# Moving seven of eight expert routings of each token tile one gather phase later

## The reference, cut to what matters

```
scores = q . sub_keys            # per token, 8 heads, two halves of 128 keys
top_s, top_i = top_k(scores, 16) # per half
cand = top_s[0] + top_s[1]       # 16 x 16 candidates
best_s, best_j = top_k(cand, 16) # 16 experts of a head
experts = i1 * 128 + i2 ; gates = softmax(best_s)
act = gelu(h . u_tab[experts])   # 128 experts of a token
x += sum_k gates * act * v_tab[experts]
```

## Time and profile before

| | us |
|---|---|
| median of 3 runs | 1702.29 (1701.94 to 1702.77) |
| span of the profiled execution | 1697.8 |
| its own time | not given apart from the span; the median lies 4.5 above the span |
| PE busy | 1314.6 (77%) |
| DVE busy | 1285.1 (76%) |
| POOL busy | 685.6 (40%) |
| ACT busy | 319.0 (19%) |
| DMA moved | 623.23 MB, mean 367 GB/s |

### The profile page before, as it was taken

The page is one execution under the profiler, slowest core; times in us unless marked ns, Lnnn a source line. Parts: engine busy times, 40 slices in busy tenths (PEclk is TensorE's granted clock), DMA queues, the critical chain, the costliest instruction groups (busy, mean ns, idle before and its releaser), DMA issues.

```text
span 1697.8 us, 15521 instructions
## 1 busy us (share of the span) xinstructions
PE 1314.6 (77%) x4636; PEld 737.9 (43%) x4636; DVE 1285.1 (76%) x3347; ACT 319.0 (19%) x932; POOL 685.6 (40%) x791
## 2 busy tenths in 40 slices
PE   7884875877686787877878778879878778787777
PEld 6663442443354344544355434545345433333332
DVE  3835999966599987878589987978679985555555
ACT  2221111122211121212121121123121111111111
POOL 6002233586285343534332243435432334445542
PEclk9897897988798888989988989889979988999989
DMA  9007998969998899999999989999999989999997
GB/s 390 9 28 291 388 367 311 397 251 384 413 383 313 313 420 420 419 420 420 420 380 420 387 330 420 420 420 415 420 389 420 369 309 421 420 420 421 420 421 309
DMA packets 86053, 623.23 MB, mean 367 GB/s; under 512 B 9808, under 2 KB 9808, under 8 KB 10960
## 3 DMA queue, kind: packets, MB, share of 16 engines
q0 software_dynamic: 73728, 536.90, 77.8%
q1 hardware_dynamic: 12240, 85.33, 12.3%
HBM read 621.15 MB, written 1.05 MB: 366 GB/s over the span
## 4 chain that ended last, share of the span: by engine, by line
DVE 42%; DMA 23%; PE 20%; issue 4%; POOL 3%; ACT 1%; DVEq 0%; POOLq 0%; ACTq 0%
DMA slot<-experts,idx 23%; DVE slot L1041 15%; PE acc L1350 12%; DVE work L760 6%; PE PX L1293 2%; DVE work L973 2%; POOL slot L458 2%; DVE ge L760 2%; DVE xs L1061 2%; PE PB L1168 1%; DVE ex L1013 1%; PE PB L1320 1%; DVE work L848 1%; DVE ti L981 1%; DVE ti L979 1%
## 5 line engine op out<-in xcount | busy, mean ns | idle before, releaser
L1350 PE MATMUL acc<-slot,diag 128*128 128x512 f32 x1780 | 874.8, 647 | 227.6 <-ACT diag L734 227.5
L458 POOL DMA_INDIRECT slot<-experts,idx x512 | 587.9, 1148 | 970.2 <-PE acc L1350 806.2
L1041 DVE CUSTOM_DVE_ANT_0 slot<-slot,h 128x1024 f32<-128x1024 f32 x512 | 611.2, 1226 | 238.7 <-DMA slot<-experts,idx 236.9
L1350 PEld LDWEIGHTS acc<-slot,diag 128*128 128x128 f32 x1780 | 359.7, 208 | 692.8 <-issue 421.6
L734 ACT ACTIVATE diag<-cst,ge 128x128 f32<-128x128 f32 x445 | 144.1, 391 | 269.6 <-DVE ge L1056 269.6
L1320 PE MATMUL PB<-hT,ring 128*128 128x128 f32 x1024 | 126.7, 285 | 5.6 <-ACT hT L698 4.1
L1320 PEld LDWEIGHTS PB<-hT,ring 128*128 128x128 f32 x1024 | 123.3, 201 | 7.6 <-ACT hT L698 5.5
L725 ACT ACTIVATE ge<-ge 128x4 f32<-128x4 f32 x129 | 26.5, 205 | 482.9 <-DVE ge L760 481.1
L1061 DVE SCALAR_TENSOR_TENSOR xs<-slot,ge,xs 128x1024 f32<-128x1024 f32 x67 | 86.3, 1288 | 2.4
L1168 PE MATMUL PB<-ring,hT 128*128 128x256 f32 x192 | 49.8, 418 | 16.9 <-DVE work L760 16.9
L1293 PE MATMUL PX<-ring,work 128*128 128x512 f32 x96 | 47.6, 642 | 15.0 <-DVE work L950 15.0
(11 more groups left out here) (231 smaller groups left out, 1197.3 us busy)
## 6 DMA issues: line engine op xcount, KB each, us to landing
ring<-weights SPq DMA_DIRECT2D x32, 1152.0 KB, 9.8
ring<-weights SPq DMA_DIRECT2D x28, 1024.0 KB, 9.2
slot<-weights SPq DMA_DIRECT2D x12, 1024.0 KB, 21.5
slot<-experts,idx POOLq DMA_INDIRECT x512, 14.9
sml<-small SPq DMA_DIRECT2D x2, 1160.0 KB, 9.2
xs<-x SPq DMA_DIRECT2D x2, 512.0 KB, 7.9
out<-xs SPq DMA_DIRECT2D x4, 256.0 KB, 5.2
tabp<-tabs SPq DMA_DIRECT2D x2, 268.0 KB, 7.9
```

Of the source, the lines that this page charges most:

```text
L458: pool.indirect_dma_start(out=slot[:, E % SLOTS, :], out_offset=None, in_=experts, in_offset=bass.IndirectOffsetOnAxis(ap=idx[:, n % 2, e: ...
L1041: ins = dve.tensor_tensor_reduce(u, u, h2[:, n % 2, :], 1.0, 0.0, ALU.mult, ALU.add, d[:, i:i + 1])
L1350: ins = pe.matmul(acc[:, half, :], diag[:, d % DIAGS, :], slot[:, E % SLOTS, D + half * 512:D + half * 512 + 512], start=(E % PICKS == 0), ...
```

## The change

`MIX1` ends with `route0`. The routings 1 to 7 of step n are placed at the beginning of phase n, ahead of the mixing of step n+1. For step 1 they carry `tab4` to `tab7` and `bT` with them (`ROUTES1`), so these run in phase 1. In phases 0 to 2 all rows are now placed within the first LEAD = 27 quads and the last five quads have none. In phase 3 the seven routings stand in quads 0, 2, 5, 8, 11, 14 and 17 (`ROUTE_AT`).

```diff
-        ("out0",), ("out1",), ("out2",), ("out3", "x1"), ("h2T", "rp"), ("route0",), ("route1",),
-        ("route2", "tab4"), ("route3", "tab5"), ("route4", "tab6"), ("route5", "tab7"), ("route6", "bT"),
-        ("route7",))
+        ("out0",), ("out1",), ("out2",), ("out3", "x1"), ("h2T", "rp"), ("route0",))
 ROUTES = tuple((f"route{h}",) for h in range(1, PH))
+
+ROUTES1 = (("route1",), ("route2", "tab4"), ("route3", "tab5"), ("route4", "tab6"), ("route5", "tab7"),
+           ("route6", "bT"), ("route7",))
+ROUTE_AT = (0, 2, 5, 8, 11, 14, 17)
+LEAD = QUADS - 5
...
-        if n == 0:
-
-            rows = [(0, r) for r in ROUTES] + [(1, r) for r in MIX1]
-        else:
-            rows = [(n + 1, r) for r in MIX + ROUTES] if n + 1 < STEPS else []
+
+        rows = [(n, r) for r in (ROUTES1 if n == 1 else ROUTES)]
+        if n + 1 < STEPS:
+            rows += [(n + 1, r) for r in (MIX if n else MIX1)]
...
-            while at < len(rows) * (quad + 1) // QUADS:
+            due = min(len(rows), len(rows) * (quad + 1) // LEAD) if n + 1 < STEPS else sum(q <= quad for q in ROUTE_AT)
+            while at < due:
```

## The result

The changed kernel takes **1717.72 us** (median of four runs, 1711.07 to 1722.77), the kernel before 1702.12 in the same session (1699.90 to 1702.77). The ratio is 1.0093, 95% interval 1.0068 to 1.0119: slower by 15.6 us, where 14 us less were forecast. Every run after is above every run before. The profiled execution is the run of 1722.77, with a span of 1721.0 us, 23.2 above the span before; that run is the slowest of the four, so the medians say 15.6 and the two traces 23.

A forecast was written before the change was run, and what follows sets the result against it. No engine passes 77%, so DMA time lost below 420 GB/s decides: 88.9 us instead of 103.6, 14.7 less, span 1683.1 from 1697.8, plus 4.5 for the median: 1687.6, said as 1688 us; own range 1679 to 1696, overall 1668 to 1702.

The forecast's parts named there:

- The removed run of phase 0: End of phase 0: one routing, then five bare quads keep DMA full, so the loss of 23.8 us goes to 0.
- The start of phase 0, and tab0 to tab3: New bare quads 0 and 13 cut the start's loss from 21.7 to 17.3 us; the tab0 to tab3 stretch keeps 20.7.
- The runs at the start of phases 1 and 2: Routings at each phase's start leave DMA idle: 18 us in phase 1 with tab4 to tab7, 11 in phase 2.
- The tighter mixing: Phases 1 and 2: 24 rows in 21 quads, so three quads hold two rows, delaying PE's additions; 6.5 us per phase.
- quad 26: h2T, rp0, then the scores and next rp in one quad: addition starts 5 us later; 3 us more per phase.
- quad 13: PE's y waits for the same quad's back rotation, with qkv3 behind it; 3 us per phase, ends 0 and 6.
- quad 20: Turn of heads 6 and 7 waits for DVE, with two quads, 20 us, in flight; 0.5 us per phase.
- Phase 3: Seven routings two or three quads apart stay DMA-paced: loss 0, old 16.6 us goes; five more chunks lengthen it 14 us.
- rival C: The gain is spent in phase 3: each routing there idles DMA 2 us, 14 come back, 1702 us; chance 0.08.
- B: Six quads with two rows in phases 1 and 2 idle DMA 7 us each: 1717; turning at 4.6; chance 0.10.
- All three conditions: Phase 3 windows below 410 GB/s; a POOL gather waiting much over 20 us at quad 13, 20 or 26; phase 1 dip over 24.
- A: Quads with two rows cost nothing and the POOL pieces hide: losses fall to 69 us, time 1668; chance 0.22.

The follow-up runs named there:

- single rows: The change, with phases 1 and 2 laid out one row a quad from quad 7 on (route7 and normA still share quad 6): 1688.51 us, ratio 0.9923.
- the first experiment: Against the kernel before, only step 3's seven routings moved into phase 3; phase 2 has mixing alone, one row a quad: 1689.85 us, ratio 0.9931.

## Why the prediction was wrong

**The removed run of phase 0: right.** 23.8 to 0 was forecast; the window 500 to 565 has 420 GB/s, and the end of the phase, 545, came at 545.62.

**The start of phase 0, and tab0 to tab3: nearly right.** 17.3 and 20.7 were forecast; 351 GB/s over 120 us are 19.7, and 21.3. The phase lost 44.4 where 40.4 was forecast; the 4 us did not show in its end.

**The runs at the start of phases 1 and 2: place right, size too small.** 18 and 11 were forecast, 25.5 and 15.4 measured. Quad 0 took 23.8 us from weights to weights at phase 1 and 23.3 at phase 2, where 19.9 was worked out, though its drain waits no more, as forecast; those 3.4 us are most of the 4.4 that the plain run lost beyond the 11. They lie in the dots: the last of the four ends 12.1 us after the weights at phase 2 and 11.8 at phase 1, where 8.9 was taken, with 5.8 and 4.7 us of waiting for landings between them. Why the gathers land that late there stays open. And such a run is moved by the change, not taken away: the three of before lost 23.8, 11.9 and 16.6, together 52.3; those of after, with all that phase 3 loses, 25.5, 15.4 and 9.8, together 50.7. The timeline of DVE in the kernel after, at the drain and at the CAST beside the coefficient pieces, and that of POOL beside the CAST:

```profile
558.10 1.41 DVE L764 TENSOR_TENSOR xs<-xs,acc 128x512 f32<-128x512 f32 x2
...
598.66 6.27 DVE L1007 CAST tif<-ti 128x32 f32<-128x32 uint32 x1
```

```profile
598.40 2.05 POOL L435 TENSOR_TENSOR work<-rot 128x512 f32<-128x512 f32 x2
...
602.43 2.47 POOL L435 TENSOR_TENSOR rot<-rot,work 128x512 f32<-128x512 f32 x2
```

The CAST of the earlier trace rows is there again with 6.27 us. The Trainium skill ("SBUF — State Buffer", section "SBUF: two separate sides") says that whichever of the two starts first gets the shared port pair for its whole instruction and the other fully blocks; the pair of 2.35 us beside two dots agrees. The CAST agrees in kind, but it did not take its turn behind one instruction: it ends only with the last of six GpSimd operations in a row, 598.40 to 604.90. The prediction's "in turn" is not what this row shows. The sum by that rule to the letter was 10 us above mine for the pieces. The run came out 7.5 above, but plain runs were 4.3 above as well, and taking the pieces out of the run gave 12.0 where I had taken 10, so the surplus that is theirs is nearer 2 than 10.

**The tighter mixing: here the prediction failed.** The step that failed is the price of "PE must finish both before it adds the last quad's experts and frees slots", put at 3 (quad 26), 3 (quad 13) and 0.5 (quad 20) per phase, 13 in all. Undoing it alone gives 29.2. By place, for both phases together: quad 13 had 6 and costs 14.3; quad 20 had 1 and costs 11.4; the last had 6 and costs 3.5, the remainder of the 29.2. The mechanism stood in the text, but quad 13 costs 7.2 a phase, above even its far end of 6, and the sizes were taken from the wrong row: the 4.90 us that PE waited for `y` at the earlier trace rows was the wait in a quad of its own. What counts in a doubled quad is when DVE has the first row's output, which is behind the four dots of the quad. PE then waits 12.01, and the additions behind it cannot start in the quad in which they are due. For quad 20 I wrote that two quads in flight, 20 us, cover it; with the additions held over a quad only one is in flight, by the count of slots (twelve, less four waiting for their addition and four of the quad at work). Its additions began behind a wait of 7.16 us, at 833.34, in the kernel after:

```profile
831.33 1.00 PE L1237 MATMUL PB<-cst,work 128*128 128x128 f32 x2 [7.16 <-DVE work L921]
833.34 6.95 PE L1354 MATMUL acc<-slot,diag 128*128 128x512 f32 x10
```

Those ten took 695 ns each, where the twelve of the quad before, at 814.38, took 5.42 us, 452 each: the granted clock was 0.57 from 833.4 to 839 and 1.00 from 814.4 to 819.8. So part of the price is a slower PE behind its own wait. How large a part no run separates: the products that keep PE busy were tried in phase 3 alone.

**Phase 3: put at 0, and not 0.** 9.8 were lost in that execution, 5.4 to 9.1 in the other kernels, where the 5.3 of before were the tail of the old run and went with it. So the routings cost 5 to 10 us there, more than the 0 taken and less than the 14 of rival C. Putting the routings elsewhere changes nothing. The phase's 10 us beyond its forecast are these.

**Added up.** Measured idle against forecast: phase 0 44.4 against 40.4, phase 1 41.5 against 28.6, phase 2 33.2 against 19.9, phase 3 9.8 against 0. That is 40.0 more than the 88.9, and 1683.1 + 40.0 = 1723.1, 2.1 above the span; of that, 2.0 is what the kernel before loses beyond the 103.6 that the forecast counted. Of the 40, quads 13, 14, 20, 21, 26 and 27 are 14.5 (16.2 and 17.8 measured in the two phases, against 10.6 and 8.9), the runs 11.9, phase 3 9.8 and phase 0 4.0. By the medians it is much the same split: 30.1 us between forecast and result, 16.2 of them the doubled quads (29.2 against 13), the other 13.9 what single rows miss of the 1674.6 that the forecast has without them. Against the 14.7 that were to be gained, the first half alone gives 1.5 us of loss and the second 0.8 of gain, neither of which could be told from no change: it took both to make the kernel slower by 15.6.

**The rivals.** B was right in its mechanism and too high in its price: 42 us by six quads, 7 each, against 29.2 measured, 4.9 each on the mean. That its 1717 is the measured time is luck: its 12.8 us too many stand in for the 13.9 that the rest of the forecast missed. Its turning point of 4.6 each rested on a gain of 27.7 without doubled quads; the measured one is 13.6, so the sign turned at 2.3 each. I gave it 0.10, because phases "held full rate through attention rows, each with its own chain". They did, with an addition after each chain; no row of before showed two chains without one. All three conditions under which the forecast was to be wrong are met: 402 GB/s in phase 3, 25.5 us at phase 1, and a gather that waited 23.52 us, at quad 26. But that longest wait stands at the cheap quad; the 20.05 of quad 13 is only at the mark and the 14.93 of quad 20 below it, so the second sign would have pointed to the wrong place:

```profile
915.41 0.94 POOL L462 DMA_INDIRECT slot<-experts,idx  x1 [23.52 <-PE acc L1354]
```

A, for which the doubled quads cost nothing, fell with them; C fell with the first experiment.

## What to carry to other kernels

When two chained pieces of work share one place (here a quad) of an in-order program, the wait in front of the second is not the wait that it showed alone: it is the time until the producer engine has passed everything that this place puts ahead of it. Before packing rows tighter, look up what frees the buffers and try that instruction between them; 18 of 29 us came back with this alone. It has to be tried place by place: ahead of `h2T` and `rp` the same step cost 10 us. And moving a run of heavy steps moves its loss with it: moved and packed, the kernel went from 1702 to 1718; moved and spread, with the GpSimd pieces spread too, to 1683.

## What the runs showed of the hardware

- With twelve buffers of 1 MiB, a pause of 14.52 us in the issue of gathers cost no rate at one place (418 GB/s), one of 20.14 there cost 5.9 us of DMA time, one of 14.93 at quad 20 4.3, and one of 23.52 at quad 26 5.2. The length of the pause does not give the cost.
- GpSimd arithmetic costs DMA time where DVE is not the limit too: in bare quads it made phase 0 lose 17.9 us more, and during the 14.5 us of `tab5` the engine issued no gather.
- A DVE CAST of 0.18 us took 6.27 beside six GpSimd operations in a row, and ended only with the last of them.
- The granted clock of TensorE was 0.50 (1.2 of 2.4 GHz) right after PE had stood idle for 16.71 us at the head of phase 3, as the window and PE's timeline of the kernel after show:

```profile
1392.00:1396.00 4.00, 3.32 (x4) 1.50 (x5) 3.97 (x8) 1.28 (x4) 0.00 (x0) 0.50 1.02 424
```

```profile
1392.68 7.59 PE L1354 MATMUL acc<-slot,diag 128*128 128x512 f32 x11 [16.71 <-ACT diag L738]
```

  Products that keep PE busy behind the routing quads raised the granted clock of the phase from 0.90 to 0.97 and changed nothing in the time.
- The changed kernel's four runs spread over 11.7 us, those of before over 2.9 in that session and 6.6 in one of nineteen runs; the four runs with steps 2 and 3 moved spread over 2.0. The profiled run of the changed kernel lies 5 us above its median. Why some of these kernels repeat less well is not shown.
